# An encoder step with product-key experts: gathers that carry two expert slots of 64 tokens, and weighted sums as two 128x64 column tiles

## The chip, the cores and the metric

The kernel runs on one core of a Trainium2 chip. The metric is the device time of one execution in microseconds (us); lower is better. The engines named below are TensorE (PE, its weight loads as PEld), VectorE (DVE), ScalarE (ACT), GpSimd (POOL, which issues the gathers) and SyncE (SP, which issues the other transfers).

## The reference, cut to what matters

One layer over 1024 new tokens and 32 tokens of a running stream: latent attention beside a short convolution, and then a feed-forward part in which every token picks 8 x 16 = 128 of 16384 single-neuron experts. All data is float32. The change concerns the expert part:

```python
def block(xb):                                   # 128 tokens
    q = (xb @ w_peer_q).reshape(PEER_BLOCK, PEER_HEADS, 2, PEER_DQ // 2)
    s = jnp.einsum('thcd,hcnd->thcn', q, peer_keys, ...)
    s_top, i_top = lax.top_k(s, PEER_TOPK)       # 16 of 128 keys, twice per head
    ...
    best, sel = lax.top_k(cand, PEER_TOPK)       # 16 of the 256 sums
    experts = jnp.take_along_axis(cand_idx, sel, axis=-1)
    g = jax.nn.softmax(best, axis=-1)
    u = peer_u[experts]
    a = jax.nn.gelu(jnp.einsum('thkd,td->thk', u, xb), approximate=False)
    v = peer_v[experts]
    return jnp.einsum('thk,thkd->td', (g * a).astype(v.dtype), v)
```

## The kernel before

Tokens are worked on in 8 tiles of 128 (t = 0 to 7) and a last tile of 32 (the running stream). For each tile there are two programs that every engine interleaves by hand, in an order that is written out in the code:

- The front of a tile, 128 numbered steps: norms, the projections by 128-column weight blocks (`in_block`, steps 4 to 27), attention (steps 29 to 62), the output product (steps 67 to 73), and from step 80 the 16 query blocks with the top-16 searches on DVE that give each head's 16 expert numbers and gates (a step of head h is `BLOCK_STEP[IN_BLOCKS + 2 * h + 1] + n`; for head 0 the sum's first part is 82).
- The slots of a tile, k = 0 to 127, one expert of each of the 128 tokens. POOL gathers row k of `peer_uv` (u and v, 8 KB a token, 1.05 MB a gather) into one of RING = 6 buffers; DVE takes the dot product of u with the token's `hf_peer` (L1240); ACT applies Gelu (L936), multiplies by the gate and writes the result on the diagonal of a 128x128 matrix `diag` (both L810); PE adds diag times v to `acc` (L785, two products of 512 columns). Then the ring buffer is free and POOL may issue gather k + 6.

While the slots of tile t run, the engines do steps 94 to 127 of tile t's own front during slots 0 to 33 and steps 0 to 93 of tile t+1 during slots 34 to 127. PE and SP do the step of slot k right after that slot; DVE and ACT do it LAG = 2 slots later. Every engine is in order, so whatever waits holds all that stands behind it. The weight blocks stream through two buffers `wst` (SP, L382), each reloaded when PE has used it; block 4 stays in the buffer `w_kept`. Between tiles, DVE copies `hf_front` to `hf_peer` (L1232), and PE starts `acc` anew with x (`take_x`, L776) once DVE has copied the old sum out (L1250). The gathers of a tile's first 16 slots take their numbers from `idx_lead`, which is a buffer of its own so that they can start before the tile ahead is done. The 32-token tile has its slots packed four to a gather and runs last, alone.

Of the kernel before, what the change touches and what calls it, by code (L numbers as in the profile page):

```python
# [21 lines left out]
P = 128  # L22
# [26 lines left out]
KEPT = (4,)  # L49
STREAMED = [b for b in range(BLOCKS) if b != NARROW and b not in KEPT]  # L50
WBUF = 2
assert len(STREAMED) % WBUF == 0
# [3 lines left out]
PSLOTS = SLOTS // PACK  # L56

# [11 lines left out]
FS_FIRST = 90  # L69
# [67 lines left out]
def build(nc, a):  # L137
    with ExitStack() as ctx:
# [23 lines left out]
        w_kept = [sb(f"w_kept{b}", KC * P) for b in KEPT]  # L162
# [5 lines left out]
        hf_peer = sb("hf_peer", D)  # L168
# [23 lines left out]
        ident = sb("ident", P)  # L192
        fold = sb("fold", DEC)
# [40 lines left out]
        s_kept = sem("s_kept_loaded")  # L234
# [74 lines left out]
        s_pack = sem("s_packed")  # L309
        s_dot = sem("s_dot")  # L310
# [11 lines left out]
        act_p = Count(sem("s_act_peer"), 2 * SLOTS)  # L322
# [7 lines left out]
        def block_view(b):  # L330

            w = w_narrow if b == NARROW else w_kept[KEPT.index(b)] if b in KEPT else wst[STREAMED.index(b) % WBUF]
            return w[:, :].rearrange("p (k n) -> p k n", k=KC)
# [40 lines left out]
        def _(sp):  # L374
            def load_block(t, b):

                i = STREAMED.index(b)
                if i >= WBUF:
                    sp.wait_ge(s_wused, BLOCKS * t + STREAMED[i - WBUF] + 1)
                elif not first(t):  # L380
                    sp.wait_ge(s_wused, BLOCKS * t - BLOCKS + STREAMED[i - WBUF] + 1)
                sp.dma_start(wst[i % WBUF][:, :], a["w_blocks"][b - (b > NARROW)]).then_inc(s_w[i % WBUF], 16)  # L382
# [47 lines left out]

            for w, b in zip(w_kept, KEPT):
                sp.dma_start(w[:, :], a["w_blocks"][b - (b > NARROW)]).then_inc(s_kept, 16)

# [15 lines left out]

            def body(t):  # L450
                for k in range(SLOTS):
# [26 lines left out]
        def _(pool):  # L478
# [16 lines left out]
            def gathers(tile, before, n):  # L495

                for k in range(n):
# [4 lines left out]
                    if g >= RING:  # L502

                        wait_apart(pool, s_slot, g - RING + 1)
                    src = idx_pack if sample(tile) else idx_lead if k < LEAD else idx_peer
                    pool.indirect_dma_start(ring[g % RING][:, :], None, a["peer_uv"],  # L506
                                            bass.IndirectOffsetOnAxis(ap=src[:, k:k + 1], axis=0)
# [9 lines left out]
        def _(pe):  # L517
# [3 lines left out]
            def w_ready(t, b):  # L521
                if b in STREAMED:
                    i = STREAMED.index(b)
                    pe.wait_ge(s_w[i % WBUF], 16 * ((len(STREAMED) // WBUF) * t + i // WBUF + 1))
                elif first(t):
                    if b == NARROW:
                        pe.wait_ge(s_narrow, 16)
                    else:
                        pe.wait_ge(s_kept, 16 * len(KEPT))

            def in_block(t, b):
                w_ready(t, b)
                w = block_view(b)
# [67 lines left out]
            def front(t, k):  # L601
                n = S_TILE + 2 if sample(t) else t
                if k == 3:
                    pe.wait_ge(s_h, t + 1)
                    if first(t):
# [141 lines left out]
                for b in range(PQ_BLOCKS):  # L747
                    if k == BLOCK_STEP[IN_BLOCKS + b]:
# [6 lines left out]
                        w = block_view(IN_BLOCKS + b)  # L755
# [12 lines left out]

            def take_x(t):
# [9 lines left out]

            def slot(t, k, n, rows):  # L780
                g = SLOTS * t + k
                pe.wait_ge(s_diag, g + 1)
# [25 lines left out]
        def _(act):  # L808
# [122 lines left out]
            def slot(t, before, k, gates, eye, rows):  # L931
                if k % TOPK == 0:

                    act.wait_ge(s_gate, PH * (t + 1) if sample(t) else PH * t + k // TOPK + 1)
                act.wait_ge(s_dot, before + k + 1)
                act_p.link(act, act.activation(dots[:, k:k + 1], dots[:, k:k + 1], ACT.Gelu))  # L936
                act_p.link(act, copy(dots[:, k:k + 1], dots[:, k:k + 1], gates[:, k:k + 1]))

                if before + k >= 2:
                    act.wait_ge(s_slot, before + k - 1)  # L940
                copy(diag[:, (k % 2) * P:(k % 2) * P + rows], eye, dots[:, k:k + 1]).then_inc(s_diag, 1)
# [12 lines left out]
            def body(t):  # L954
                act_p.start(t)
                for k in range(SLOTS + LAG):
                    if k < SLOTS:
# [415 lines left out]
```

## Time and profile before

| | us |
|---|---|
| median of three runs | 3679.81 (3675.72 to 3700.01) |
| the profiled execution | 3673.75 |
| its span, first to last instruction | 3672.0 |
| PE busy in it | 3157.0 (86%) |
| DVE busy | 2254.3 (61%) |
| ACT busy | 1723.2 (47%) |
| POOL busy | 1166.2 (32%) |
| moved by the transfers | 1281.22 MB, of which gathers 1107.36 MB |

A PE that is busy 86% of the span can still be waited for all the time or none of it; what counts is which engine is full in which stage of a tile. A tile takes some 422 us. The tile used below has its first dot product at 1409 us and is read in four stretches: slots 0 to 33 (the top-16 searches), 34 to about 63 (the input blocks), about 64 to 100 (attention), and the rest (output product and the first query blocks).

### The profile page before, as it was taken

The page shows a single profiled execution, that of the slowest core. Times are in us where ns is not written, and L with a number is a line of the kernel's source. Part 1 is how long each engine was busy: PE and PEld are TensorE (multiplying, and loading weights), DVE is VectorE, ACT ScalarE, POOL GpSimd, SP SyncE. Part 2 cuts the span into 40 slices and gives each one's busy share as a digit, 9 for nine tenths or more (in the row PEclk, how much of TensorE's full clock was granted, in tenths as well). Part 3 has the DMA queues.
Part 4 walks back from the last instruction along what each step waited for, and adds up shares of the span by engine and source line. Part 5 has one row for each costly group of instructions (what it writes and reads, how often), then busy time and mean ns, then how long its engine had stood idle before and what let it go on. Part 6 is the DMA issues. An engine that isn't in the chain of part 4 may idle for free.

```text
span 3672.0 us, 41426 instructions
## 1 busy us (share of the span) xinstructions
PE 3157.0 (86%) x12316; PEld 1803.3 (49%) x12316; DVE 2254.3 (61%) x5824; ACT 1723.2 (47%) x4378; POOL 1166.2 (32%) x1071
## 2 busy tenths in 40 slices
PE   7679988899879997899888998899978998789876
PEld 5446544455446544465444544465444654365441
DVE  2684558555684558645685557845586456835674
ACT  2343744445444644446344554437444454446333
POOL 1232332333333332333333233333333332323233
PEclk9899998999999999999999999999999999999989
DMA  6699999999899999999999999999999998979878
GB/s 212 263 343 352 351 377 351 360 360 368 351 369 367 351 362 362 359 372 363 363 360 349 355 357 362 380 350 365 368 357 362 350 359 339 378 275 367 329 281 356
DMA packets 204668, 1281.22 MB, mean 349 GB/s; under 512 B 26304, under 2 KB 27872, under 8 KB 69280
## 3 DMA queue, kind: packets, MB, share of 16 engines
q0 software_dynamic: 152064, 1107.36, 78.2%
q1 hardware_dynamic: 52384, 171.22, 12.3%
q8 instruction: 102, 1.67, 0.2%
q14 instruction: 118, 0.97, 0.1%
HBM read 1272.39 MB, written 5.55 MB: 348 GB/s over the span
## 4 chain that ended last, share of the span: by engine, by line
PE 47%; DVE 30%; DMA 12%; ACT 6%; issue 5%; DVEq 0%; POOL 0%; SPq 0%; POOLq 0%; ACTq 0%
PE acc L785 25%; DVE ring L1240 10%; DMA wst<-in_w_blocks 6%; PE Sps L559 5%; DMA ring<-in_peer_uv,idx_peer 4%; PE Sps L697 3%; PE M L715 3%; PE M L543 2%; PE T L519 2%; DVE bufA L1013 2%; DVE bufA L1204 2%; DVE eab L1206 2%; PE Sps L596 2%; DVE bufA L1202 2%; DMA ring<-in_peer_uv,idx_pack 1%
## 5 line engine op out<-in xcount | busy, mean ns | idle before, releaser
L785 PE MATMUL acc<-ring,diag 128*128 128x512 f32 (+1 forms) x4224 | 2066.1, 622 | 336.8 <-ACT diag L810 335.0
L506 POOL DMA_INDIRECT ring<-in_peer_uv,idx_peer x896 | 985.9, 1100 | 1966.8 <-PE acc L785 1809.0
L1240 DVE CUSTOM_DVE_ANT_0 ring<-ring,hf_peer 128x1024 f32<-128x1024 f32 x1024 | 1234.7, 1219 | 341.5 <-DMA ring<-in_peer_uv,idx_peer 331.3
L785 PEld LDWEIGHTS acc<-ring,diag 128*128 128x128 f32 (+1 forms) x4224 | 764.8, 195 | 1238.0 <-issue 698.4
L810 ACT ACTIVATE diag<-ident,dots 128x128 f32<-128x128 f32 x1024 | 411.2, 402 | 466.6 <-PE acc L785 443.3
L936 ACT ACTIVATE dots<-dots 128x1 f32<-128x1 f32 x1056 | 210.2, 199 | 851.1 <-DVE dots L1240 846.4
L810 ACT ACTIVATE dots<-dots,gate_peer 128x1 f32<-128x1 f32 x1024 | 301.5, 294 | 33.3
L758 PEld LDWEIGHTS M<-actT,wst 128*128 128x128 f32 x2304 | 289.2, 200 | 42.4 <-issue 40.3
L758 PE MATMUL M<-actT,wst 128*128 128x128 f32 (+1 forms) x2304 | 292.8, 283 | 2.6 <-DMA wst<-in_w_blocks 1.8
L506 POOL DMA_INDIRECT ring<-in_peer_uv,idx_lead x128 | 134.6, 1051 | 468.6 <-PE acc L785 291.7
L936 ACT ACT_TABLE_LOAD x192 | 246.3, 1283 | 61.3 <-DVE dots L1240 58.1
L559 PEld LDWEIGHTS Sps<-actT,wst 128*128 128x128 f32 x1728 | 217.0, 200 | 86.2 <-DMA wst<-in_w_blocks 54.7
L559 PE MATMUL Sps<-actT,wst 128*128 128x128 f32 (+1 forms) x1728 | 223.0, 285 | 41.8 <-DMA wst<-in_w_blocks 41.7
L1133 DVE CUSTOM_DVE_ANT_0 bufA<-Sps,mask 128x1024 f32<-128x1024 f32 (+1 forms) x64 | 73.0, 1141 | 135.6 <-PE Sps L697 135.6
L519 PE MATMUL T<-ident,bufA 128*128 128x128 f32 x585 | 85.3, 289 | 52.7 <-ACT bufA L810 44.5
L715 PEld LDWEIGHTS M<-vv,bufB 128*128 128x128 f32 x944 | 115.5, 192 | 30.2 <-issue 29.6
L990 DVE RECIPROCAL st<-st 128x1 f32<-128x1 f32 x63 | 10.2, 162 | 188.4 <-ACT st L815 158.3
L519 PEld LDWEIGHTS T<-ident,bufA 128*128 128x128 f32 x585 | 72.9, 149 | 100.2 <-ACT bufA L810 51.2
L715 PE MATMUL M<-vv,bufB 128*128 128x64 f32 x944 | 112.3, 271 | 0.0
L697 PE MATMUL Sps<-kT,qT 96*128 96x512 f32 (+1 forms) x240 | 111.9, 585 | 0.0
L896 ACT ACTIVATE bufA<-bufA,nm 128x1024 f32<-128x1024 f32 (+1 forms) x64 | 69.3, 1083 | 76.9 <-DVE nm L1136 76.8
L1099 DVE TENSOR_TENSOR uT<-Sps,csb 128x128 f32<-128x128 f32 x36 | 10.5, 292 | 152.3 <-ACT csb L810 152.3
(182 smaller groups left out, 2591.7 us busy)
## 6 DMA issues: line engine op xcount, KB each, us to landing
wst<-in_w_blocks SPq DMA_DIRECT2D x288, 512.0 KB, 7.7
ring<-in_peer_uv,idx_peer POOLq DMA_INDIRECT x896, 8.2
x_front<-in_x_p SPq DMA_DIRECT2D x8, 512.0 KB, 11.8
w_out_sb<-in_w_out SPq DMA_DIRECT2D x8, 512.0 KB, 5.9
o_y_p<-qT SPq DMA_DIRECT2D x8, 512.0 KB, 8.3
ring<-in_peer_uv,idx_lead POOLq DMA_INDIRECT x128, 9.0
w_uq_sb<-in_w_uq SPq DMA_DIRECT2D x3, 384.0 KB, 6.1
w_ukv_sb<-in_w_ukv SPq DMA_DIRECT2D x2, 512.0 KB, 8.1
```

The costliest lines, as they stand in the source:

```text
L506: pool.indirect_dma_start(ring[g % RING][:, :], None, a["peer_uv"], bass.IndirectOffsetOnAxis(ap=src[:, k:k + 1], axis=0)).then_inc(s_g[g ...
L519: return pe.transpose(dst, src, ident[:, :])
L543: mm = pe.matmul(bank[:, at:at + n], actT_v[:, c, :], w[:, c, 0:n], start=(c == 0), stop=(c == KC - 1))
L559: mm = pe.matmul(bank[:, part * P:part * P + n], w[:, c, :], actT_v[:, c, 0:n], start=(c == 0), stop=(c == KC - 1))
L596: mm = pe.matmul(bank, actT_v[:, 4 * mixer + c, :], w_out_v[:, 4 * mixer + c, half * 512:(half + 1) * 512], start=(c == 0), stop=(c == 3))
L697: mm = pe.matmul(Sps[:, lo:lo + n_keys], qT[0:QK, h * P:(h + 1) * P], kT_v[0:QK, h, lo:lo + n_keys], start=True, stop=True)
L715: mm = pe.matmul(M1[:, h * VD:(h + 1) * VD], bufB[:, c * P:(c + 1) * P], vv[:, (c * H + h) * VD:(c * H + h + 1) * VD], start=(c == 0), sto ...
L758: mm = pe.matmul(Mb[b % 2][:, 0:n], w[:, c, :], actT_v[:, c, 0:n], start=(c == 0), stop=(c == KC - 1))
L785: mm = pe.matmul(acc[0:rows, half * 512:(half + 1) * 512], diag[:, (k % 2) * P:(k % 2) * P + rows], ring[g % RING][:, D + half * 512:D + ( ...
L810: return act.activation(out, in_, ACT.Copy, scale=scale)
L936: act_p.link(act, act.activation(dots[:, k:k + 1], dots[:, k:k + 1], ACT.Gelu))
L1240: dve.tensor_tensor_reduce(u, u, hf[:, :], 1.0, 0.0, ALU.mult, ALU.add, dots[:, k:k + 1]).then_inc(s_dot, 1)
```

## The change

- A gather of the eight large tiles now serves 64 tokens and two slots: partition q * 64 + i holds slot q's expert of token i of one token half j. Slots 2m and 2m+1 of the program are such a pair (j = 0, 1). The count and the size of the gathers stay.
- DVE's dot products take the features from `hf_half[j]`, which holds the 64 tokens of half j twice. SP fills both by four transfers from `hf_front` at the head of a tile's slots (`hand`), in place of DVE's copy.
- ACT works on a pair at a time: one Gelu for two columns, two gate multiplications, two 128x64 matrices (`fold2` is the identity of 64 stacked twice).
- PE works on a pair at a time: four products with 64 stationary columns, alternating between output partitions 0-63 and 64-127 (column tile 0 and 1). The ring buffers of a pair are released together.
- The expert numbers and gates of a head are turned to the new layout by four small products on PE (step + 8), and DVE copies them from PSUM (step + 9); before, DVE wrote the numbers at step + 5 and the gates at step + 7.
- Block 4 streams like the others; the first tile's front is run to step 91 (before: 89) ahead of its slots; the scratch for gather descriptors is halved.

```diff
-KEPT = (4,)
-STREAMED = [b for b in range(BLOCKS) if b != NARROW and b not in KEPT]
+STREAMED = [b for b in range(BLOCKS) if b != NARROW]
+def pair_of(g):
+    return g // 2 if g < SLOTS * TILES else PAIRS * TILES + g - SLOTS * TILES
+def packed_col(k):
+    return k // TOPK * TOPK + k % 2 * (TOPK // 2) + k % TOPK // 2
-FS_FIRST = 90
+FS_FIRST = 92
...
@@ SP
+            def hand(t):
+                sp.wait_ge(s_hf, t + 1)
+                if not first(t):
+                    sp.wait_ge(s_dot, SLOTS * t)
+                for j in range(2):
+                    for q in range(2):
+                        sp.dma_start(hf_half[j][q * HALF_T:(q + 1) * HALF_T, :],
+                                     hf_front[j * HALF_T:(j + 1) * HALF_T, :]).then_inc(s_handh, 16)
...
@@ POOL, gathers
-                        wait_apart(pool, s_slot, g - RING + 1)
+                        wait_apart(pool, s_slot, pair_of(g - RING) + 1)
...
@@ PE, front
+                for h in range(0 if sample(t) else PH):
+                    if k == BLOCK_STEP[IN_BLOCKS + 2 * h + 1] + 8:
+                        pe.wait_ge(s_gate, PH * t + h + 1)
+                        if h >= 2:
+                            pe.wait_ge(s_idx, PH * t + h - 1)
+                        own = head_own[:, :].rearrange("p (y q i) -> p y q i", y=2, q=2)
+                        for q in range(2):
+                            rows = slice(q * HALF_T, (q + 1) * HALF_T)
+                            packed = Tb[h % 2][rows, 0:2 * TOPK].rearrange("p (y j i) -> p y j i", y=2, j=2)
+                            for j in range(2):
+                                mm = pe.matmul(packed[:, :, j, :], ident[:, j * HALF_T:(j + 1) * HALF_T], own[:, :, q, :],
+                                               start=True, stop=True)
+                        mm.then_inc(s_headps, 1)
...
@@ PE, slots
+            def pair(t, m):
+                pe.wait_ge(s_diag, PAIRS * t + m + 1)
+                for j in range(2):
+                    g = SLOTS * t + 2 * m + j
+                    pe.wait_ge(s_g[g % RING], 16 * (g // RING + 1))
+                for half in range(2):
+                    for j in range(2):
+                        at = ((m % 2) * 2 + j) * HALF_T
+                        mm = pe.matmul(acc[j * HALF_T:(j + 1) * HALF_T, half * 512:(half + 1) * 512],
+                                       diag[:, at:at + HALF_T],
+                                       ring[(SLOTS * t + 2 * m + j) % RING][:, D + half * 512:D + (half + 1) * 512],
+                                       start=False, stop=(m == PAIRS - 1))
+                mm.then_inc(s_slot, 1)
...
                 for k in range(SLOTS):
-                    slot(t, k, SLOTS, P)
+                    if k % 2:
+                        pair(t, k // 2)
...
@@ ACT
+            def pair(t, m):
+                if m % (TOPK // 2) == 0:
+                    act.wait_ge(s_idx, PH * t + m // (TOPK // 2) + 1)
+                act.wait_ge(s_dot, SLOTS * t + 2 * m + 2)
+                act_p.link(act, act.activation(dots[:, 2 * m:2 * m + 2], dots[:, 2 * m:2 * m + 2], ACT.Gelu))
+                for j in range(2):
+                    c = packed_col(2 * m + j)
+                    weighted = copy(dots[:, 2 * m + j:2 * m + j + 1], dots[:, 2 * m + j:2 * m + j + 1], gate_peer[:, c:c + 1])
+                act_p.link(act, weighted)
+                if PAIRS * t + m >= 2:
+                    act.wait_ge(s_slot, PAIRS * t + m - 1)
+                for j in range(2):
+                    at = ((m % 2) * 2 + j) * HALF_T
+                    spread = copy(diag[:, at:at + HALF_T], fold2[:, :], dots[:, 2 * m + j:2 * m + j + 1])
+                spread.then_inc(s_diag, 1)
...
@@ DVE
-                        dve.tensor_copy(dst, pabf[:, 0:TOPK]).then_inc(s_idx, 1)
+                    if k == BLOCK_STEP[IN_BLOCKS + 2 * h + 1] + 9 and not sample(t):
+                        dve.wait_ge(s_headps, PH * t + h + 1)
+                        dve.tensor_copy(gate_peer[:, h * TOPK:(h + 1) * TOPK], Tb[h % 2][:, TOPK:2 * TOPK])
+                        dve.tensor_copy((idx_peer if h else idx_lead)[:, h * TOPK:(h + 1) * TOPK],
+                                        Tb[h % 2][:, 0:TOPK]).then_inc(s_idx, 1)
...
-                dve.tensor_copy(hf_peer[:, :], hf_front[:, :]).then_inc(s_handh, 1)
...
             def body(t):
-                hand(t)
+                dve.wait_ge(s_handh, 64 * (t + 1))
                 for k in range(SLOTS + LAG):
                     if k < SLOTS:
-                        slot(t, k, hf_peer)
+                        slot(t, k, hf_half[k % 2])
```

What stands on PE in the attention stage before: one slot, or two, between pieces of a head's attention (scores L697, transposes L519, values L715).

```order
L785 MATMUL acc<-ring1,diag 128x512 x2
L697 MATMUL Sps<-kT,qT 128x512 x2
L785 MATMUL acc<-ring2,diag 128x512 x2
L715 MATMUL M1<-vv,bufB 128x64 x8
L785 MATMUL acc<-ring3,diag 128x512 x2
L785 MATMUL acc<-ring4,diag 128x512 x2
L519 MATMUL T0<-ident,bufA 128x128 x4
L519 MATMUL T1<-ident,bufA 128x128 x4
```

And in the change (L819 is the pair, L714 the scores, L732 the values, L537 the transposes):

```order
L714 MATMUL Sps<-kT,qT 128x512 x2
L732 MATMUL M1<-vv,bufB 128x64 x8
L819 MATMUL acc<-ring4,diag 64x512
L819 MATMUL acc<-ring5,diag 64x512
L819 MATMUL acc<-ring4,diag 64x512
L819 MATMUL acc<-ring5,diag 64x512
L537 MATMUL T0<-ident,bufA 128x128 x4
L537 MATMUL T1<-ident,bufA 128x128 x4
```

Two slots always stand together, and the front pieces of two slots stand together behind them.

DVE at the end of a tile before, from the write of the next tile's first expert numbers (`idx_lead`) to the tile's third dot product from the last:

```order
L1208 SCALAR_TENSOR_TENSOR pabf<-eab 128x16
L1214 CAST idx_lead<-pabf 128x16
L1240 ISA ring4,dots<-ring4,hf_peer 128x1024
L1240 ISA dots 128x1
L1011 MAX tv<-Sps 128x8
L1012 MAX_INDEX ti<-tv,Sps 128x8
L1013 MATCH_REPLACE bufA<-tv,Sps 128x128
L1014 MAX tv<-bufA 128x8
L1015 MAX_INDEX ti<-tv,bufA 128x8
L1240 ISA ring5,dots<-ring5,hf_peer 128x1024
```

The same engine in the change, at the tile's last dot product:

```order
L1298 ISA ring1,dots<-ring1,hf_half1 128x1024
L1298 ISA dots 128x1
L1283 COPY gate_peer<-T0 128x16
L1284 CAST idx_lead<-T0 128x16
L1250 TENSOR_TENSOR bufA<-tv 128x256
L1253 CAST tif<-ti 128x32
```

The write of `idx_lead` has moved from ahead of the last four dot products to behind the last one.

## Rows read from the trace of the kernel before

**Rows 1.** The page, busy time by engine

```profile
PE 3157.0 (86%) x12316; PEld 1803.3 (49%) x12316; DVE 2254.3 (61%) x5824; ACT 1723.2 (47%) x4378; POOL 1166.2 (32%) x1071
```

**Rows 2.** The chain that ended last, by engine

```profile
PE 47%; DVE 30%; DMA 12%; ACT 6%; issue 5%; DVEq 0%; POOL 0%; SPq 0%; POOLq 0%; ACTq 0%
```

**Rows 3.** Waits: engine, what for, total us, times, longest

```profile
POOL ring L506 <- PE acc L785: 2141.5, 839, 12.8
```

**Rows 4.** One tile in four stretches: PE, PEld, DVE, ACT, POOL busy; clock, DMA share, GB/s

```profile
1409.00:1522.00 113.00, 86.78 (x313) 48.37 (x314) 97.23 (x307) 54.97 (x143) 35.38 (x31) 0.92 0.89 348
1522.00:1633.00 111.00, 101.84 (x486) 65.97 (x485) 49.71 (x110) 43.26 (x121) 36.02 (x32) 0.97 0.94 368
1633.00:1737.00 104.00, 101.92 (x382) 55.09 (x381) 59.77 (x108) 70.69 (x154) 38.17 (x38) 1.00 0.95 360
1737.00:1831.00 94.00, 81.09 (x263) 42.40 (x260) 57.87 (x150) 37.08 (x106) 31.32 (x30) 0.95 0.95 368
```

**Rows 5.** The same stretches, L785 alone: PE and PEld busy, with counts

```profile
1522.00:1633.00 111.00, 59.82 (x128) 22.91 (x127) 0.97 0.94 368
1633.00:1737.00 104.00, 70.38 (x148) 25.66 (x146) 1.00 0.95 360
1737.00:1831.00 94.00, 55.51 (x113) 21.66 (x112) 0.95 0.95 368
```

**Rows 6.** Windows of 5 us at a tile's end, columns as in rows 4

```profile
970.00:975.00 5.00, 5.00 (x26) 3.34 (x25) 4.41 (x17) 1.96 (x7) 1.86 (x2) 1.00 1.01 418
990.00:995.00 5.00, 5.00 (x10) 2.06 (x9) 2.08 (x7) 2.67 (x10) 0.00 (x0) 0.71 0.02 7
```

**Rows 7.** PE's timeline: start us, us, what

```profile
1015.40 3.60 PE L785 MATMUL acc<-ring,diag 128*128 128x512 f32 x8
1018.84 1.95 PE L758 MATMUL M<-actT,wst 128*128 128x128 f32 x16
```

**Rows 8.** PE's timeline around the products with 64 stationary columns (L579)

```profile
753.58 1.88 PE L785 MATMUL acc<-ring,diag 128*128 128x512 f32 x4
755.39 3.71 PE L579 MATMUL T<-qT,w_ukv_sb 128*64 128x128 f32 x32
759.03 1.98 PE L785 MATMUL acc<-ring,diag 128*128 128x512 f32 x4
760.85 1.95 PE L559 MATMUL Sps<-actT,wst 128*128 128x128 f32 x16
```

**Rows 9.** Groups by shape: weight loads of L579 (busy us, mean ns, idle before)

```profile
L579 PEld LDWEIGHTS T<-qT,w_ukv_sb 128*64 128x64 f32 x288 | 31.2, 137 | 6.2 <-issue 6.1
```

**Rows 10.** The chain in order of time: the first gather, issue to landing

```profile
125.68 5.65 DMA ring<-in_peer_uv,idx_lead
```

**Rows 11.** Timeline of all engines: a slot's release, another's dot product to PE

```profile
1003.03 1.88 PE L785 MATMUL acc<-ring,diag 128*128 128x512 f32 x4
...
1005.73 1.42 POOL L506 DMA_INDIRECT ring<-in_peer_uv,idx_lead  x1 [2.57 <-PE acc L785]
...
1009.29 1.22 DVE L1240 CUSTOM_DVE_ANT_0 ring<-ring,hf_peer 128x1024 f32<-128x1024 f32 x1
...
1010.79 0.29 ACT L810 ACTIVATE dots<-dots,gate_peer 128x1 f32<-128x1 f32 x1
...
1011.12 0.40 ACT L810 ACTIVATE diag<-ident,dots 128x128 f32<-128x128 f32 x1
...
1011.57 0.70 PE L785 MATMUL acc<-ring,diag 128*128 128x512 f32 x1 [2.12 <-ACT diag L810]
```

**Rows 12.** DVE's timeline at a tile's end

```profile
967.24 0.17 DVE L1214 CAST idx_lead<-pabf 128x16 uint32<-128x16 f32 x1
...
974.98 1.21 DVE L1240 CUSTOM_DVE_ANT_0 ring<-ring,hf_peer 128x1024 f32<-128x1024 f32 x1
...
985.12 0.67 DVE L1232 COPY hf_peer<-hf_front 128x1024 f32<-128x1024 f32 x1
```

**Rows 13.** Transfers, KB each and median us from issue to landing

```profile
bufA<-hf_front SPq DMA_DIRECT2D x4, 128.0 KB, 4.0
```

More of the change, by code:

```diff
@@ L167, in build @@
         hf_front = sb("hf_front", D)
-        hf_peer = sb("hf_peer", D)
+        hf_half = [sb(f"hf_half{j}", D) for j in range(2)]
         idx_s = sb("idx_s", SLOTS, U32)
@@ L604, in front @@
                     pe.wait_ge(s_h, t + 1)
+                    if not first(t):
+                        pe.wait_ge(s_idx, PH * t)
                     if first(t):
@@ L929, in front, with slot @@
                                        accum_out=gsum[:, h:h + 1]).then_inc(s_ge, 1)
[L931 to L934 removed]
+            def pair(t, m):
[13 more added lines that the diff above has]
+                spread.then_inc(s_diag, 1)
+            def slot(k):
+                before = SLOTS * TILES
                 act.wait_ge(s_dot, before + k + 1)
                 act_p.link(act, act.activation(dots[:, k:k + 1], dots[:, k:k + 1], ACT.Gelu))
[L937 to L941, printed above, removed]
+                act_p.link(act, copy(dots[:, k:k + 1], dots[:, k:k + 1], gate_pack[:, k:k + 1]))
+                act.wait_ge(s_slot, PAIRS * TILES + k - 1)
+                copy(diag[:, (k % 2) * P:(k % 2) * P + DEC], fold[:, :], dots[:, k:k + 1]).then_inc(s_diag, 1)
             def finish(t):
@@ L956, in body @@
                 for k in range(SLOTS + LAG):
-                    if k < SLOTS:
-                        slot(t, SLOTS * t, k, gate_peer, ident[:, :], P)
+                    if k < SLOTS and k % 2:
+                        pair(t, k // 2)
                     if k == 1 and not first(t):
@@ L976, in _ @@
             for k in range(PSLOTS):
-                slot(S_TILE, SLOTS * TILES, k, gate_pack, fold[:, :], DEC)
+                slot(k)
                 if k == 1:
@@ L1226, in whole_front @@
                     dve_f.end()
-            def hand(t):
-                dve.wait_ge(s_hf, t + 1)
-                if not first(t):
-                    dve.wait_ge(s_dot, SLOTS * t)
-                dve.tensor_copy(hf_peer[:, :], hf_front[:, :]).then_inc(s_handh, 1)
-                dve.wait_ge(s_handh, t + 1)
             def slot(t, k, hf):
@@ L1287, in _ @@
                 dve.tensor_copy(fold[group, :], ident[group, group]).then_inc(s_fold, 1)
+            for q in range(2):
+                group = slice(q * HALF_T, (q + 1) * HALF_T)
+                dve.tensor_copy(fold2[group, :], ident[group, group]).then_inc(s_fold2, 1)
             body(0)
```

59 lines of the change are left out of this document (29 added, 30 removed).

## The prediction

> **What bounds the kernel now.** Start with the page: PE is busy 86%, no other engine over 61% [rows 1], and PE is also the largest part of the chain that ended last, with DVE second [rows 2]. The waits say the same: POOL spends 2141.5 us, in 839 waits, on PE freeing a ring buffer [rows 3]. An average hides the stages, so the next view is one tile cut in four [rows 4]. The three late stretches hold 128, 148 and 113 records of L785 [rows 5], four to a slot, so 32, 37 and 28 slots; the first holds the other 32 or so.
>
> - Searches (113 us): DVE is busy 97.23 us of 113. DVE bounds this stretch; PE has 26 us to spare.
> - Input blocks (111 us, 3.47 us a slot): PE is busy 101.84.
> - Attention (104 us, 2.81 us a slot): PE is busy 101.92, so here PE alone sets the pace.
> - Output product and first queries (94 us, 3.36 us a slot): PE 81.09.
>
> Then the transfers. They show a share of 0.89 to 0.95 in these stretches, at 348 to 368 GB/s [rows 4]. That looks full, but is not: with gathers piled up the same engines move 418 GB/s [rows 6]. A gather of 1.05 MB therefore costs 2.5 us of transfer time. That is the floor behind PE, 11% under attention's 2.81 us.
>
> **PE's part of a pair.** Eight records of L785 start 3.44 us apart from the next line (1015.40 to 1018.84) [rows 7]: 0.43 us a record, 1.72 us a slot, 3.44 a pair. The 592 to 700 ns that a record shows is its modelled end. The changed pair has eight records too, two for each product, in the order A A B B A A B B over the column tiles A and B. No two column tiles ever work side by side in the trace of before, so this has to be bounded. Full overlap would be four record times, 1.72 us; none, 3.44. I take a value between: if records start in program order and two of one tile cannot overlap, the second A runs with the first B, the second B with the third A, and so on, which makes 5 record times, 2.15 us. To this comes the change between full products and 64-column products. L579 is such a 64-column group: the slot ahead of it takes 1.81 us instead of 1.72, the slot after it 1.82 (753.58 to 755.39, 759.03 to 760.85) [rows 8], and its own 32 records 3.64 us. So 0.1 us in and 0.1 to 0.2 out, 0.3 a pair: 2.45 us.
>
> The Trainium skill, TensorEngine Tiling (Array Packing), Key Properties, says that tiles execute weight loads and matmuls in parallel and that a change of tiling mode drains the engine. The second agrees with the 0.1 us seen at L579; the first no run here shows yet. By its table of theoretical speedup (2x at 64 columns or fewer) the pair would cost 1.72 + 0.3 us, which would take another 0.4 us a pair off PE and nothing off the floor of the transfers.
>
> **Attention.** PE's own work there is 101.92 less 37 x 1.72 = 38.3 us, 1.04 a slot, 2.1 a pair. PE's demand falls from 5.5 to 4.5 us a pair and is then under the transfers' 5.0. What remains is the ring: six buffers were six chances, now they are three pairs. The round of a pair without any queue: release to issue 0.8 us (1004.91 to 1005.73) [rows 11]; first gather 5.65 [rows 10]; second 2.5 behind it; its dot product to PE's start 2.28 (1009.29 to 1011.57) [rows 11]; a second gate copy, 0.29, and a second matrix of half the width, at most 0.40, say 0.6 together [rows 11]; PE 2.45. Sum 14.3 us for six slots, 2.4 a slot, below the 2.5 of the transfers. Waits come on top: PE in the middle of front work, 2.1 us of it a pair, so some 0.6; a reload of ACT's function table behind the softmax; DVE with its own front. I allow 1.6 us: 15.9 us, 2.65 a slot. 37 x 0.16 = 6 us saved.
>
> **Output product and first queries.** 28 slots; PE's own share is 81.09 - 28 x 1.72 = 33 us, 1.2 a slot, near attention's. The same 0.16 to 0.18 a slot gives 5 us. A part of this stretch is a chain of norms through four engines, which a lighter PE does not shorten.
>
> **Input blocks.** It moves 368 x 111 = 40.8 MB, 98 us at 418 GB/s. Block 4 adds 0.52 MB, 1.3 us, and one more turn of two `wst` buffers in a stretch in which PE waits for weights. So the gain is between 12 us and a loss of 4; I take 2 saved, near the low end, since the weights' turn is no PE time.
>
> **Searches and the tile's end.** DVE bounds, so PE's relief is worth nothing here. DVE gets two copies of 16 columns and loses a cast and the 0.67 us copy [rows 12]: some 0.2 x 8 heads, 1 us. PE waits for a gate one step ahead of DVE's, eight times a tile, while the transfers stand queued; hidden. Pairing takes a slot's time of the slack that landed gathers have in front of DVE; 1 us of starvation.
> The hand-over needs more care. SP may issue the four transfers once the last dot product is done (976.2). DVE then still has 9 us of searches before the copy at 985.12 [rows 12]. Four transfers of 256 KB: 2.5 us at the full rate, 5 at half, plus the latency of the nearest row, 4.0 us for 128 KB from the same buffer [rows 13]; 5 to 9 us in all. The 9 us hide it; without that cover each tile would pay it in full. On SP the weight loads of steps 95 and later stand behind it, and these wait for PE's use of an earlier block anyway.
> `idx_lead` moves from 967.24 to behind the last dot product, near 976.6: 9 us later. POOL stands still and the transfers run dry for that time. But at present they run dry behind it: 7 GB/s at 990 to 995 [rows 6], six full buffers waiting for DVE and `take_x`. Issued at 977.5, the first gather lands 5.65 us later, up to 2.5 more for the hand-over, 983 to 986, when DVE first wants it. I take nothing, between 2 us gained and 6 lost. Stretch: 2 us lost.
>
> **Elsewhere.** The first tile's front has two more steps ahead of the slots, the same work at another time. Halved scratch: six gathers at most are in flight as before; nothing. Gelu once a pair is ACT time, and ACT bounds nothing.
>
> **Sum.** +2 - 2 - 6 - 5 = -11 us a tile, times 8 = -88 us. 3673.75 - 88 = 3586 for an execution like the profiled one, which is 6 us below the median: 3590 us, 2.4% faster.
>
> **Rivals.**
> 1. The transfers take all (0.10). Waits in the ring stay under 0.7 us, and every stretch but the first runs at 418 GB/s: 113 + 99 + 37 x 2.5 + 83 = 388 us a tile for 422, times 8 = 272 us saved, 3400. For it: a share of 0.95 at only 360 GB/s. Against it: three pairs, in-order engines.
> 2. The ring of three pairs eats it (0.14). If waits cost 2.6 us a round and not 1.6, the round is 16.9 us, 2.81 a slot, exactly attention's present pace. With +2 for the searches: 3690, no change.
> 3. Slower (0.22): the column tiles run one after the other. Then PE's pair is 3.44 + 0.3 = 3.74 us; attention needs 5.8 us a pair, 2.91 a slot and 4 us more a stretch; input blocks and the last stretch lose about 4 each, as batches of two find PE just as full and wait longer; searches 4 to 6 with the starts at the tile's end; 16 to 18 us a tile, 130 to 150 in all: 3800 to 3825. It decides from about 3.1 us a pair upward, since there PE again needs what it needs now.
>
> A page rule would lead there by another way. The Trainium skill, TensorE: Matmul & The Clock Gate, Part 3, says that weight loads overlap running matmuls only in another row group, and both column tiles here use all rows. Against it stands L579: its weight loads take 137 ns [rows 9] and its 32 records still start 0.11 us apart [rows 8], with the same rows in use. If each of the eight records paid its 137 ns, the pair would be 2.45 + 1.1 = 3.55 us; this rule is part of rival 3's 0.22, I give it 0.04.
>
> Inside the 0.54 that are left for the forecast lies one more doubt, the granted clock: the searches have 0.92, a mix of its levels of 2.4 and 1.2 GHz, at a PE that is 77% busy, attention 1.00 (2.4 GHz) at 98% [rows 4]. PE would be 75% busy in all stretches. Eight per cent on 300 us of PE work a tile is 24 us, spread over waits that are there anyway; it pulls towards rival 2.
>
> **How the numbers follow.** Forecast 0.54 (3480 to 3643), rival 1 0.10, rival 2 0.14, rival 3 0.22. A measurement of this kernel tells about 1% from no change, 37 us. Faster is the forecast and rival 1, less a small part of the forecast: 0.62. Same: rival 2 and that rest, 0.16. Slower 0.22. The range leaves out rival 1's better half and rival 3's worse: 3430 to 3810.
>
> **What would show it.** In the changed trace: a pair's eight records take 2.1 to 2.5 us from the first start to the next line's (3.4 or more is rival 3). Attention at 2.6 to 2.7 us a slot, PE below 85% busy in it, the transfers at 375 GB/s or more. At a tile's end the last dot product and the next tile's first should stay 10 to 11 us apart, with the four transfers landed in between; over 13 us and the hand-over or `idx_lead` is exposed. The searches at 113 to 117 us. What would make it wrong: serial column tiles, or a ring in which PE and the transfers both idle.

## The result

The change makes the kernel slower: 3780.19 us median (3772.17 to 3789.2) against 3685.53, a ratio of 1.0254 (95% interval 1.0209 to 1.0299). The forecast was 3590 us.

The page of the changed kernel, busy time by engine, and its chain that ended last:

```profile
PE 2674.7 (71%) x12828; PEld 1422.3 (38%) x12828; DVE 2268.3 (60%) x5882; ACT 1456.1 (39%) x3849; POOL 1171.7 (31%) x1071
```

```profile
DMA 29%; PE 29%; DVE 25%; issue 9%; ACT 6%; POOL 2%; SPq 0%; DVEq 0%; POOLq 0%; ACTq 0%
```

PE's busy time fell from 3157.0 us [rows 1] by 482 us, in a longer span. In the chain PE went from 47% to 29% and the transfers from 12% to 29% [rows 2]. So the relief of PE is real, and the kernel's end comes later all the same.

Its waits (engine, what for, total us, times, longest):

```profile
POOL ring L524 <- PE acc L819: 1884.6, 415, 19.9
DVE ring L1298 <- DMA ring<-in_peer_uv,idx_peer: 788.0, 486, 6.3
DVE ring L1298 <- DMA hf_half<-hf_front: 56.2, 7, 8.9
```

DVE's waits for gathers in the kernel before, beside POOL's 2141.5 us [rows 3]:

```profile
DVE ring L1240 <- DMA ring<-in_peer_uv,idx_peer: 331.3, 236, 6.4
```

DVE now waits 788 us for gathers, where it waited 331. PE waits 702.6 us for the matrices of ACT (L856), where it waited 335.0 (L810). POOL waits for PE's release 12% less than before, although PE's busy share is 71% and no longer 86%. Engines that wait for one another in a circle, none of them full, point to a ring with too few places; the runs below test it.

The same tile as in rows 4 (t = 3), cut at the same slots (PE, PEld, DVE, ACT, POOL busy; clock, DMA share, GB/s):

```profile
1444.00:1560.00 116.00, 71.21 (x362) 35.16 (x363) 98.30 (x313) 45.42 (x126) 32.25 (x30) 0.78 0.90 355
1560.00:1675.00 115.00, 88.20 (x490) 56.63 (x488) 48.82 (x109) 35.63 (x103) 30.98 (x30) 0.88 0.89 350
1675.00:1778.00 103.00, 79.47 (x378) 39.16 (x374) 60.49 (x108) 59.28 (x134) 40.44 (x38) 0.91 0.96 369
1778.00:1878.00 100.00, 67.18 (x278) 29.14 (x278) 58.60 (x150) 32.08 (x95) 35.13 (x31) 0.84 0.92 344
```

Attention takes 103 us for 104 [rows 4], with PE busy 79 us in it and not 102. The starts of DVE's dot products (L1240 before, L1298 after), averaged over tiles 1 to 6, divide a tile's length. The last column is from a tile's last dot product to the next tile's first, averaged over all seven tile ends:

| us | tile | slots 0-34 | 34-64 | 64-100 | 100-127 | last to first |
|---|---|---|---|---|---|---|
| before | 423.0 | 112.0 | 112.2 | 103.7 | 84.2 | 10.8 |
| the change | 434.5 | 115.4 | 114.4 | 103.7 | 82.7 | 18.4 |

So 11.5 us a tile: 7.6 at the tile's end, 3.4 in the searches, 2.2 in the input blocks, nothing from attention, 1.5 back in the last stretch.

These averages leave out the last large tile (t = 7), whose front work is that of the 32-token tile. From its first dot product to its last it takes 475.6 us before and 505.7 in the change: 30 us more, of which 15.5 lie in slots 34 to 64 and 10.3 in slots 64 to 100. The two profiled executions differ by 110 us; 69 of these are lost in tiles 1 to 6, 30 in this one tile, 7.6 at the end of tile 0 and 3 behind the last dot product of tile 7. The first dot product comes 8 us later, and tile 0 is 8 us shorter.

PE's timeline in attention shows what a pair costs now:

```profile
1305.12 1.94 PE L819 MATMUL acc<-ring,diag 128*64 128x512 f32 x8
1306.99 1.09 PE L537 MATMUL T<-ident,bufA 128*128 128x128 f32 x8
1310.17 1.94 PE L819 MATMUL acc<-ring,diag 128*64 128x512 f32 x8 [2.09 <-ACT diag L856]
```

Eight records in 1.87 us (1305.12 to 1306.99), against 3.44 before [rows 7]. In the single records, the starts come in four couples, 0.007 us apart inside a couple and 0.43 to 0.48 us from one couple to the next. So the two column tiles run side by side, better than I had it. Ahead of its next pair PE waits 2.09 us.

The end of the same tile that rows 12 show, on DVE, POOL and SP:

```profile
990.21 1.20 DVE L1298 CUSTOM_DVE_ANT_0 ring<-ring,hf_half 128x1024 f32<-128x1024 f32 x1
...
991.43 0.16 DVE L1284 CAST idx_lead<-T 128x16 uint32<-128x16 f32 x1
...
1000.26 0.28 DVE L1076 FIND_INDEX8 ti<-tv,bufA 128x8 uint32<-128x128 f32 x1
1008.45 1.23 DVE L1298 CUSTOM_DVE_ANT_0 ring<-ring,hf_half 128x1024 f32<-128x1024 f32 x1 [7.90 <-DMA hf_half<-hf_front]
```

```profile
992.49 0.94 POOL L524 DMA_INDIRECT ring<-in_peer_uv,idx_lead  x1 [14.75 <-DVE idx_lead L1284]
...
998.81 0.94 POOL L524 DMA_INDIRECT ring<-in_peer_uv,idx_lead  x1 [0.31 <-issue]
```

```profile
992.68 2.83 SPq L463 DMA_DIRECT2D hf_half<-hf_front  x4
```

Windows of 5 us there:

```profile
990.00:995.00 5.00, 4.38 (x28) 2.63 (x26) 4.38 (x18) 2.55 (x6) 1.90 (x3) 1.00 0.34 93
...
1000.00:1005.00 5.00, 0.00 (x0) 0.00 (x0) 0.40 (x3) 0.00 (x0) 0.00 (x0) 0.50 1.02 283
1005.00:1010.00 5.00, 0.00 (x0) 0.00 (x0) 1.55 (x3) 0.00 (x0) 0.00 (x0) 0.50 1.01 325
```

The transfers run nearly dry until 995 (93 GB/s), because POOL waits 14.75 us for the expert numbers. Then POOL issues six gathers between 992.49 and 998.81, while SP issues the four hand-over transfers from 992.68 on, and both share the engines. DVE, which waits for the hand-over, starts 16 us after its first issue (1008.45): it has 9 us of searches, then nothing for 7.9 us. From 1000.5 to 1008.4 no engine computes.

### The profile page after: what moved, and what is told of

The parts are those of the page before. It is cut to its first block, busy times and chain, and to the rows that moved or that the text cites. A ratio compares the mean times of both kernels' runs of the same rounds, so it can differ in the third digit from the quotient of the medians.

```text
span 3781.7 us, 41104 instructions
## 1 busy us (share of the span) xinstructions
PE 2674.7 (71%) x12828; PEld 1422.3 (38%) x12828; DVE 2268.3 (60%) x5882; ACT 1456.1 (39%) x3849; POOL 1171.7 (31%) x1071
## 4 chain that ended last, share of the span: by engine, by line
DMA 29%; PE 29%; DVE 25%; issue 9%; ACT 6%; POOL 2%; SPq 0%; DVEq 0%; POOLq 0%; ACTq 0%
DMA ring<-in_peer_uv,idx_peer 16%; PE acc L819 13%; DMA wst<-in_w_blocks 8%; DVE ring L1298 8%; PE Sps L574 5%; DMA hf_half<-hf_front 3%; POOL ring L524 2%; PE M L558 2%; ACT diag L856 2%; DVE bufA L1265 1%; DVE bufA L1074 1%; DVE eab L1267 1%; DVE bufA L1263 1%; DMA ring<-in_peer_uv,idx_pack 1%; PE Sps L714 1%
## 5 line engine op out<-in xcount | busy, mean ns | idle before, releaser
L1298 DVE CUSTOM_DVE_ANT_0 ring<-ring,hf_half 128x1024 f32<-128x1024 f32 x1024 | 1245.6, 1221 | 861.4 <-DMA ring<-in_peer_uv,idx_peer 788.0
L819 PE MATMUL acc<-ring,diag 128*64 128x512 f32 x4096 | 1251.1, 742 | 703.9 <-ACT diag L856 702.6
L819 PEld LDWEIGHTS acc<-ring,diag 128*64 128x64 f32 x4096 | 295.7, 161 | 1261.2 <-ACT diag L856 830.7
L982 ACT ACTIVATE dots<-dots 128x2 f32<-128x2 f32 x512 | 103.8, 203 | 1298.0 <-DVE dots L1298 1277.1
L574 PE MATMUL Sps<-actT,wst 128*128 128x128 f32 (+1 forms) x1728 | 254.4, 308 | 91.5 <-DMA wst<-in_w_blocks 90.5
L856 ACT ACTIVATE diag<-fold,dots 128x64 f32<-128x64 f32 (+1 forms) x1056 | 310.7, 340 | 19.8 <-PE acc L830 2.2
L856 ACT ACTIVATE dots<-dots,gate_peer 128x1 f32<-128x1 f32 x1024 | 245.7, 287 | 16.8
L537 PE MATMUL T<-ident,bufA 128*128 128x128 f32 x585 | 94.2, 308 | 85.9 <-DVE st L1051 40.1
L732 PEld LDWEIGHTS M<-vv,bufB 128*128 128x128 f32 x944 | 118.4, 197 | 42.1 <-issue 30.8
L537 PEld LDWEIGHTS T<-ident,bufA 128*128 128x128 f32 x585 | 73.3, 158 | 151.2 <-ACT bufA L942 53.3
L558 PE MATMUL M<-wst,actT 128*128 128x128 f32 x720 | 104.2, 305 | 33.2 <-DMA wst<-in_w_blocks 24.9
L714 PE MATMUL Sps<-kT,qT 96*128 96x512 f32 (+1 forms) x240 | 122.8, 632 | 0.0
L732 PE MATMUL M<-vv,bufB 128*128 128x64 f32 x944 | 117.7, 278 | 3.8 <-ACTq L946 3.8
L558 PEld LDWEIGHTS M<-wst,actT 128*128 128x128 f32 x720 | 95.8, 214 | 56.5 <-DMA wst<-in_w_blocks 32.8
L807 PE MATMUL acc<-x_front,ident 128*128 128x512 f32 (+1 forms) x36 | 30.0, 981 | 112.8 <-DVE qT L1308 112.8
```

The lines of the kernel that those rows point to most:

```text
L537: return pe.transpose(dst, src, ident[:, :])
L558: mm = pe.matmul(bank[:, at:at + n], actT_v[:, c, :], w[:, c, 0:n], start=(c == 0), stop=(c == KC - 1))
L574: mm = pe.matmul(bank[:, part * P:part * P + n], w[:, c, :], actT_v[:, c, 0:n], start=(c == 0), stop=(c == KC - 1))
L714: mm = pe.matmul(Sps[:, lo:lo + n_keys], qT[0:QK, h * P:(h + 1) * P], kT_v[0:QK, h, lo:lo + n_keys], start=True, stop=True)
L732: mm = pe.matmul(M1[:, h * VD:(h + 1) * VD], bufB[:, c * P:(c + 1) * P], vv[:, (c * H + h) * VD:(c * H + h + 1) * VD], start=(c == 0), sto ...
L819: mm = pe.matmul(acc[j * HALF_T:(j + 1) * HALF_T, half * 512:(half + 1) * 512], diag[:, at:at + HALF_T], ring[(SLOTS * t + 2 * m + j) % RI ...
```

## The experiments

Every time is a median of device times, and every ratio is to the kernel before, run on the same chip. The kernel before had medians of 3687 us beside e1 to e4, 3683 beside e5 to e8, and 3689 beside e9 to e12. The ratios on record are not exactly the quotients of the medians; where the two lead to different sizes, both are given. The stage columns are those of the profiled execution, read as in the table above. The code of each run is cut to its main lines.

| run | us | ratio (95% interval) | tile | 0-34 | 34-64 | 64-100 | 100-127 | last to first |
|---|---|---|---|---|---|---|---|---|
| e1_hand_once | 3720.34 | 1.0097 (1.0057 to 1.0136) | 425.7 | 115.4 | 113.9 | 103.7 | 82.5 | 10.3 |
| e2_lead_early | 3819.39 | 1.0352 (1.0325 to 1.0379) | 439.8 | 115.3 | 114.8 | 103.1 | 83.7 | 22.6 |
| e3_both | 3733.49 | 1.0109 (1.0069 to 1.0148) | 426.6 | 115.3 | 114.6 | 103.4 | 82.9 | 10.4 |
| e4_ring8_after | 3589.60 | 0.9722 (0.9696 to 0.9748) | 412.8 | 114.6 | 112.0 | 90.0 | 76.0 | 20.6 |
| e5_ring8_before | 3664.24 | 0.9936 (0.9907 to 0.9964) | 422.2 | 112.1 | 114.0 | 102.4 | 82.9 | 10.8 |
| e6_pair_release | 3743.42 | 1.0138 (1.0100 to 1.0176) | 431.6 | 112.6 | 113.8 | 107.8 | 86.4 | 10.9 |
| e7_ring8_hand_once | 3539.84 | 0.9597 (0.9564 to 0.9630) | 402.2 | 114.2 | 111.6 | 90.5 | 75.5 | 10.3 |
| e8_warm | 3826.68 | 1.0355 (1.0304 to 1.0406) | 440.6 | 115.8 | 115.7 | 105.3 | 82.8 | 21.5 |
| e9_dve_hand | 3744.02 | 1.0144 (1.0110 to 1.0178) | 429.6 | 115.6 | 113.4 | 104.6 | 82.8 | 13.2 |
| e10_hand_kept | 3718.97 | 1.0100 (1.0072 to 1.0128) | 423.5 | 115.3 | 111.4 | 104.0 | 82.4 | 10.4 |
| e11_ring8_full | 3588.48 | 0.9734 (0.9720 to 0.9747) | 410.3 | 114.3 | 112.2 | 90.4 | 80.3 | 13.2 |
| e12_ring8_before_pairs | 3633.35 | 0.9848 (0.9829 to 0.9867) | 417.7 | 112.1 | 108.6 | 102.2 | 83.9 | 10.9 |

### The tile's end: the hand-over, and the expert numbers

```diff
 e1_hand_once
@@ SP body
-                hand(t)
+                if first(t):
+                    hand(t)
@@ DVE body
-                dve.wait_ge(s_handh, 64 * (t + 1))
+                if first(t):
+                    dve.wait_ge(s_handh, 64)
```

> The change, but the four transfers hf_front to hf_half are made for the first tile alone; later tiles use the first tile's features (that part of the computation is left out). Theory A (the end of a tile is what was lost): DVE's wait of 7.9 us at each of seven tile ends goes, last dot product to first falls from 18.4 to about 11 us, the whole from 3780 to about 3725 us. Theory B (the ring in pairs limits everywhere, the tile's end is refilled by it): gathers are issued no earlier, so under 20 us are won. Theory C (the lower granted clock of PE): no gain beyond A's.

Theory A held: 60 us less than the change, and from last to first dot product 10.3 us for 18.4. The run also saves the 0.67 us copy that the kernel before has at each tile's end.

```diff
 e2_lead_early
@@ POOL, gathers
+                        if k == 0:
+                            wait_apart(pool, s_lead, tile + 1)
@@ DVE, step + 5
+                        if h == 0 and not sample(t):
+                            dve.tensor_copy(idx_lead[:, 0:TOPK], head_own[:, 0:TOPK]).then_inc(s_lead, 1)
```

> The change, but the first head's 16 expert numbers are written to idx_lead at step + 5 in their old layout (so the first 16 gathers bring other experts than the layout asks for), with a semaphore of their own for POOL; the hand-over stays. Theory A: POOL's wait of 14.75 us for idx_lead falls to about 6, the transfers no longer run dry ahead of the hand-over; but the hand-over still ends 16 us after the last dot product or a little sooner, since it shares the transfer engines with fewer gathers: 20 to 30 us won. Theory B: 0 to 10 us, the six buffers are full either way when DVE starts.

A miss by both theories: 39 us slower than the change, with 22.6 us from last to first dot product. With the numbers early (POOL issues its first gather 5.7 us ahead of the last dot product, and not 2.3 us behind it), gathers are issued before SP may issue the hand-over, and at the head of tile 3 DVE starts 20.6 us after the hand-over's first issue (1440.93 to 1461.49) and not 16. Over the kernel DVE waits 92.0 us for the hand-over, and 56.2 in the change. I had reckoned only with the share of the rate that the hand-over gets, not with what is queued when it comes; that this is the reason fits the order of the issues, but no run separates it. As long as SP makes the hand-over, late expert numbers help it.

> The change with both edits, of the runs hand_once and lead_early. Theory A: the tile's end is as before the change (10.8 us from last to first dot product); what is left over the kernel before (3 to 5 us a tile in the searches and input blocks, less what attention gives) is the ring's pairs and block 4: 3690 to 3710 us. If the column tiles' 1.6 us a pair were usable anywhere, it would have to be under 3680. Theory B: 3730 or more.

3733 us, with e1's interval overlapping: without the hand-over early numbers are worth nothing (10.4 against 10.3 us at the tile's end). So the end of the tile was lost by the hand-over alone. Theory A had the tile's end right and the whole wrong: 3690 to 3710 was expected, and theory B's 3730 or more is what came. The 40 to 46 us still lost over the kernel before lie elsewhere.

```diff
 e9_dve_hand
@@ DVE body
+                for j in range(2):
+                    for q in range(2):
+                        dve.tensor_copy(hf_half[j][q * HALF_T:(q + 1) * HALF_T, :],
+                                        hf_front[j * HALF_T:(j + 1) * HALF_T, :]).then_inc(s_handh, 1)
```

> The change with the hand-over made by four copies on DVE (64 partitions x 1024, two of them from one partition half to the other) in place of SP's four transfers; everything is computed. Four times the 0.67 us of the old copy are 2.7 us at each tile's end, behind the 9 us of searches: last to first dot product 12.5 to 13.5 us instead of 18.4, 35 to 50 us less than the change: 3730 to 3745. If it were the late expert numbers that hold the tile's end, nothing is won.

As expected: 3744 us, 36 less than the change, 13.2 us. DVE's timeline has the copies, two straight and two across the partition halves. In the single records all four take 0.67 to 0.69 us, start to start 0.70 to 0.72:

```profile
1422.26 2.83 DVE L1321 COPY hf_half<-hf_front 64x1024 f32<-64x1024 f32 x4
```

### The ring

```diff
 e4_ring8_after, e5_ring8_before
-RING = 6
+RING = 8
-        w_out = sb("w_out_sb", KC * D)
+        w_out = sb("w_out_sb", KC // 2 * D)
-                                   w_out_v[:, 4 * mixer + c, half * 512:(half + 1) * 512],
+                                   w_out_v[:, c, half * 512:(half + 1) * 512],
```

> The change with a ring of 8 buffers (four pairs). For the room, w_out is half as large, and its four chunks are used for both halves of the product (that part of the computation is changed, not its time; four loads of 512 KB fewer in the first tile). Theory B (three pairs are too few): attention falls from 2.8 to 2.55 us a slot, POOL waits less for PE, the whole falls by 80 us or more, to under 3700. Theory A alone: the tile ends stay, under 30 us won. Theory C (clock): nothing.

> The kernel before with a ring of 8 single buffers, w_out halved in the same way. If three pairs are the trouble and six single buffers are enough for a PE that is the bound (theory B), this gains little: under 30 us, attention stays at 2.8 us a slot because PE is full there. If the ring is short for any kernel here (theory D: it was short before the change too), it gains about as much as the changed kernel did with its fourth pair, 150 us or more.

The two together decide it. The fourth pair takes 190 us off the changed kernel; two more single buffers take 19 us (by the ratio 24) off the kernel before. In e4 DVE's waits for gathers are down again to 271.2 us, less than in the kernel before. Attention in e4, and in e5:

```profile
1602.00:1693.00 91.00, 74.59 (x378) 37.88 (x376) 60.49 (x111) 59.23 (x133) 43.38 (x38) 0.98 0.98 400
```

```profile
1631.00:1733.00 102.00, 100.00 (x377) 54.58 (x376) 59.11 (x108) 68.44 (x150) 36.55 (x36) 1.00 0.95 355
```

In e4 attention runs at 2.50 us a slot (90.0 for 36), the figure that the prediction had as the transfers' floor. But the rate is 400 GB/s and not the 418 of [rows 6], and at 400 a gather of 1.05 MB takes 2.6 us: 90.0 us move 36.0 MB, and 36 gathers are 37.7. So I read the pace as that of the transfers (share 0.98) plus one or two gathers that had landed ahead. In e5 PE is busy 100 us of 102, and buffers can't help there. In attention the ring matters only once PE is out of the way.

```diff
 e6_pair_release (of the kernel before; e12_ring8_before_pairs is the same with e5's edit)
@@ POOL, gathers
-                        wait_apart(pool, s_slot, g - RING + 1)
+                        wait_apart(pool, s_slot, (g - RING) // 2 * 2 + 2)
```

> The kernel before with one line of POOL changed: a gather waits until both slots of the pair that held its buffer are done (the release of the change without anything else of it; PE's work stays at 1.72 us a slot, one slot at a time). Theory B: the pairwise release alone costs 60 to 150 us, since a buffer then stays held for another slot's time of 3 us in a round of 17. Theory A (only the tile's end matters): within 20 us of before.

It costs 60 us by the medians and 51 (37 to 65) by the ratio, around the lower end of theory B's figure, by one line and with no other part of the change. Attention goes from 103.7 to 107.8 us with the same work on PE, and tile 7 from 475.6 to 490.4. DVE's waits for gathers more than double by that line (331.3 before):

```profile
DVE ring L1240 <- DMA ring<-in_peer_uv,idx_peer: 706.1, 461, 7.0
```

With e1 this makes an account of the change: 3683 for the kernel before, plus 60 for the pairwise release, less 23 for all the rest (column tiles, ACT's pairs, packed numbers, block 4, and the copy that e1 saves) gives 3720, and plus 60 for the hand-over 3780. The 23 is the weak term: by the ratios it is 15, and the intervals of e6 and e1 overlap (1.0100 to 1.0176, 1.0057 to 1.0136). What is shown is that all the rest together bought little or nothing with three pairs.

> The change with the ring of 8 (w_out halved) and the hand-over for the first tile alone. If the tile's end and the ring add up (theories A and B), 60 us less than the ring of 8 alone: 3530. If with a fourth pair the wait at the tile's end is refilled by the deeper ring, under 30 us less: 3560 to 3590.

3540 us: 50 less than e4 (46 by the ratios), between the two expectations and nearer the 60 of additive effects, so a deeper ring does not refill the tile's end (20.6 us in e4, 10.3 here).

> The kernel before with a ring of 8 (w_out halved) and gathers issued only when both slots of a pair are done. Everything of the pairing's hold on the buffers, nothing of the column tiles. If the fourth pair gives back what the pairwise release takes, this is near the kernel before with 8 single buffers (3664), and the rest of the way to 3590 and 3540 is what the column tiles are worth: 75 us and more. If the pairing still costs, 3700 or more.

3633 us. Here the pairwise release costs nothing; it is even 31 us faster than eight single buffers. That was not expected, and its cause is open. What the traces show is that the gain lies in the input blocks (108.6 against 114.0 us), where PE's waits for weights fall by 25 us. The waits in e5 and in e12:

```profile
PE Sps L559 <- DMA wst<-in_w_blocks: 50.5, 31, 3.0
```

```profile
PE Sps L559 <- DMA wst<-in_w_blocks: 25.0, 25, 1.7
```

From e12 to e7 it is 93 us: that is what the column tiles and the rest of the change, without the hand-over, are worth with four pairs, against 15 to 23 with three (e6 to e1). Both differences hold some 4 us for the copy at the tile's end, which e7 and e1 leave out.

### The clock, and block 4

```diff
 e8_warm
@@ PE, pair
+                for _ in range(16):
+                    pe.matmul(acc[:, 0:P], mask_tile[:, :], zeros[:, :], start=False, stop=False)
                 pe.wait_ge(s_diag, PAIRS * t + m + 1)
```

> The change with 16 products of 128x128 zeros in bfloat16 (added to acc, which they leave as it is) ahead of PE's wait for each pair, to keep PE occupied: 8 to 9 a slot. Theory C (the granted clock of 0.84 instead of 0.955 is what costs): the clock rises to 0.93 or more and the time falls by 30 us or more, in spite of 0.9 us of added work a pair. Theory B: the clock rises and the time stays or grows by up to 40 us, since PE is not waited for long enough to matter.

The granted clock rose from 0.842 to 0.902 of full speed over the kernel, in attention from 0.91 to 0.98, and the time rose by 46 us (by the ratios 37). Theory C's 0.93 was not reached, and no gain came. So a higher clock did not bring a gain that covers 0.9 us of products a pair. What the lower clock (a mix of 1.2 and 2.4 GHz) costs by itself was not separated, and it stays a possible part of the small yield with three pairs; it does not forbid a faster kernel, since e7 is the fastest with 0.866.

```diff
 e10_hand_kept
-STREAMED = [b for b in range(BLOCKS) if b != NARROW]
+KEPT = (4,)
+STREAMED = [b for b in range(BLOCKS) if b != NARROW and b not in KEPT]
```

> The run hand_once with block 4 kept in a buffer again (for the room both halves share one feature buffer, so half of the dot products use the other half's features). If the streamed block 4 is what the input blocks lost, 2 to 4 us a tile come back: 3690 to 3705. If the ring alone limits, within 10 us of hand_once (3720).

3719 against 3720: not told apart by time, and not the 3690 to 3705 of a guilty block 4. The profiled tiles show 2.5 us less in the input blocks (111.4 against 113.9), but e10's profiled execution (3695) was the fastest of its four and e1's (3733) the second slowest of its five, so this may be the spread of executions. That block 4 costs anything is not shown.

### A whole kernel

```diff
 e11_ring8_full (with e9's copies)
+WO_BLOCKS = 4
+PQ0 = IN_BLOCKS + WO_BLOCKS
-RING = 6
+RING = 8
@@ SP
+    if IN_BLOCKS <= b < PQ0:
+        return ((25, 26, 30, 31) if first(t) else (40, 41, 70, 71))[b - IN_BLOCKS]
@@ PE, out_product
+                if mixer == 1:
+                    for pr in range(2):
+                        w_ready(t, IN_BLOCKS + 2 * half + pr)
+                        w = wst[(STREAMED.index(IN_BLOCKS + 2 * half + pr) + len(STREAMED) * t) % WBUF]
+                        for c in range(2):
+                            mm = pe.matmul(bank, actT_v[:, 4 + 2 * pr + c, :], w[:, c * 512:(c + 1) * 512],
+                                           start=(pr + c == 0), stop=(pr + c == 2))
+                        mm.then_inc(s_wused, 1)
```

> A whole kernel, everything computed: the change with DVE's hand-over copies and a ring of 8, for which half of w_out streams through the weight buffers as four more blocks of 512 KB a tile. From the ring of 8 with the hand-over once (3540): plus 2.7 us a tile for the copies, plus 2.1 MB or 5 us a tile of transfers, of which attention may hide a part: 3560 to 3600, 2.3 to 3.3% faster than the kernel before. If the added blocks stall the output product, 3640 or more.

3588.48 us, ratio 0.9734 (0.9720 to 0.9747): 2.7% faster than the kernel before and 5.1% than the change, with everything computed. (That this is also the forecast's figure is chance: the forecast was for three pairs.) Its attention takes 90.4 us (e4: 90.0), with the transfers at 394 GB/s in the profiled stretch (1595 to 1687).

The weights of the output product cost where they are used (80.3 us for e7's 75.5 in slots 100 to 127), and the copies 2.9 us at the tile's end, 7.7 us a tile together and 49 us in all; for that, attention has the fourth pair.

## Why the prediction was wrong, by its own steps

- **"What bounds the kernel now"** held. PE was the bound in attention (e5: 100 of 102 us with eight buffers and no gain), and with four pairs attention ran at 2.50 us a slot, limited by the transfers as the prediction had it. The figure fits by some luck: the rate was 394 to 400 GB/s and not 418, and landed gathers made up the difference.
- **"PE's part of a pair"**: 2.45 us predicted, 1.87 measured, with the mode changes in it. The model of five record times was too slow: the records start in couples 0.007 us apart, which makes four, 1.72 us. And the change between full and 64-column products costs 0.15 us here and not 0.3. The Trainium skill, TensorEngine Tiling (Array Packing), Key Properties and Theoretical Speedup, has tiles that work in parallel and up to 2x at 64 columns; the trace agrees, with 3.44 to 1.87, a factor of 1.84 with the mode change in it. The Trainium skill, TensorE: Matmul & The Clock Gate, Part 3, lists weight loads as overlapping running matmuls only where the row group differs (it also names a background weight buffer, of which the trace shows nothing). The trace does not bear the row group out as a limit here: these products use all rows, their weight loads take 0.137 us each, and the couples still start 0.43 us apart. An error of this size works towards a faster kernel than forecast; it is not what failed.
- **"Attention", the sum of the round, is the first step that failed.** "I allow 1.6 us: 15.9 us" for six slots; measured, over tiles 1 to 6, 17.2. By its terms: second gather's issue behind the first's 1.5, its issue to its dot product 9.4, dot product to PE 3.3, PE 1.9, release to issue 1.1. I had 8.15 for the 10.9 us of the first two: this is the term that was mis-sized. A gather lands 5.65 us after its issue in an empty kernel [rows 10], but at a transfer share of 0.96 there is no empty queue, and most of the waits that I had put on PE and ACT lie there. The trace of before had the loaded figure (the number of gathers, then the median us from issue to landing):

```profile
ring<-in_peer_uv,idx_peer POOLq DMA_INDIRECT x896, 8.2
```

  With 8.2 in the place of 5.65 the sum of 14.3 becomes 16.8, which is rival 2's 16.9 before any further wait. Rival 2 said it: at attention's present pace the relief is gone. It measured 2.88 us a slot, as before. It had 0.14 and should have had the most. e6 shows that pairwise release alone costs 4 us of attention; in the change these are earned back, which I put down to the column tiles, though no run has them alone.
- **"The 9 us hide it" is the second, and the larger in us.** The transfers were costed at 5 to 9 us. They took 16 beside six gathers issued in the same 6 us, and DVE stood still for some 8 us at each of seven ends (56.2 in all): 60 us by e1. The fault was to cost a transfer alone when the same step moved six gathers to its side. The prediction named the 9 us later `idx_lead` and its nearness to the hand-over, and then took nothing for it. It also had the sign of that interplay wrong (e2).
- **"Output product"**: 5 us predicted, 1.5 measured; the ring again, as e4's 76.0 shows.
- **"Input blocks"**: 2 us saved predicted, 2.2 lost. e6 loses 1.6 there by the pairwise release alone (113.8 against 112.2). That block 4 has a part in it was not shown (e10).
- **"Searches"**: 2 us lost predicted for stretch and end, 3.4 in the stretch alone. Neither e6 (112.6) nor e12 (112.1) has it, and every kernel with the rest of the change has 114.2 or more. So the ring is not its cause; the packing on PE, ACT's pairs and the lower clock (0.78 for 0.92) come together there and were not separated. Part of it has a name in the traces, DVE's wait for ACT's squares of the finished tile, which goes from 10.6 to 23.4 us over nine waits, 1.4 us at each tile (L1254 before, L1312 in the change).
- **The sum** took all eight tiles for alike ("times 8"). The last large tile lost 30 us and an inner one 11.5. e6 (490.4 us) has half of these 30 by the pairwise release alone, and e4 (480.4) is within 5 of the kernel before with a fourth pair, so the ring is most of it.
- **Rival 3**, slower by column tiles in a row, had the right sign for the wrong reason, and its 3800 to 3825 is 20 to 45 us above what was measured. That 3780 lies inside the stated range of 3430 to 3810 is luck: no case that the range was made of happened.

## What to carry to other kernels

Before an engine is relieved, work out the round of the ring that feeds it, with the time to landing that the trace shows under load (8.2 us here) and not that of an empty queue (5.65), and count the places as the release counts them: six buffers freed in pairs are three. Relief and ring depth are worth little apart (15 to 23 us, and 19 to 24 us here) and much together: 143 us from 3683 to 3540 where the hand-over is left out, and 100 us from 3689 to 3588 in the kernel that computes everything. And a transfer put where another queue has just been let loose costs what it has to share; if an engine can do the copy in 0.7 us, let it.

## What was not expected of the hardware

- Two products on column tiles 0 and 1, in float32, start 0.007 us apart and take the time of one: eight records of 512 columns in 1.87 us for 3.44.
- DVE copies 64 partitions x 1024 to the other half of the partitions in 0.69 us, as to the same half (0.67 to 0.69); four of them take 2.83 us.
- Issuing gathers in pairs is 31 us faster than one at a time with eight buffers (3633 against 3664) and 60 us slower with six (3743 against 3683). The cause of the first is open.
